# Query-key slabs by seven products, gate slabs drained later, and repeated waits of TensorE removed

## The reference

```python
def _mixer(h, ...):
    z = h @ w_in
    dq, dk, dv, cq, ckv, kr, gl = jnp.split(z, IN_SPLIT_IDX, axis=-1)
    ...
    o_a = _diff_attention(dq..., dk..., dv..., pos, rel_table, lam, lam_init, diff_subln_g)
    o_b = _mla(cq, ckv, kr, pos, mla_q_norm_g, w_uq, mla_kv_norm_g, w_ukv)
    g = jax.nn.sigmoid(gl + b_gate)
    g_a, g_b = g[..., :D_MODEL], g[..., D_MODEL:]
    m = g_a * (o_a @ w_branch_diff) + g_b * (o_b @ w_branch_mla)
    return m @ w_out
```

## Time and profile before

| | us |
|---|---|
| median of 3 runs | 2605.68 (2603.1 to 2606.06) |
| the profiled execution | 2605.08 |
| its span, first to last instruction | 2603.1 |
| TensorE busy | 2518.7 |
| VectorE busy | 1002.7 |
| ScalarE busy | 365.6 |
| GpSimd busy | 130.6 |
| mixer of layer 0, about | 900 to 1185 |
| mixer of layer 1, about | 1421 to 1710 |

### The profile page before, as it was taken

One profiled execution on the slowest core, in us unless ns is written; L12 is line 12 of the kernel. 1 busy time (PEld: TensorE's weight loads), 2 busy tenths in 40 slices (PEclk: granted clock), 3 DMA queues, 4 the chain that ended last, 5 costly groups with the idle time before them and its releaser, 6 DMA issues.

```text
span 2603.1 us, 74060 instructions
## 1 busy us (share of the span) xinstructions
PE 2518.7 (97%) x33806; PEld 2146.4 (82%) x33806; DVE 1002.7 (39%) x1856; ACT 365.6 (14%) x842; POOL 130.6 (5%) x114
## 2 busy tenths in 40 slices
PE   8999999999999999999999999999999999999998
PEld 8966778887698577876994778769999998999997
DVE  5663464633477734444666235440000001000002
ACT  1001241210100023401000234120000001000000
POOL 0000000000100001400000014010000000000000
PEclk9999999999999999999999999999999999999999
DMA  6445242013444542345435323579999999999996
GB/s 260 148 144 196 105 146 110 4 59 130 146 170 150 194 166 82 130 166 209 164 114 197 140 104 129 232 259 368 426 427 426 426 426 401 426 427 426 426 425 256
DMA packets 58054, 607.72 MB, mean 233 GB/s; under 512 B 7365, under 2 KB 7493, under 8 KB 12353
## 3 DMA queue, kind: packets, MB, share of 16 engines
q1 hardware_dynamic: 52272, 587.74, 56.7%
q0 software_dynamic: 5648, 18.04, 2.1%
HBM read 599.66 MB, written 6.09 MB: 233 GB/s over the span
## 4 chain that ended last, share of the span: by engine, by line
PE 90%; DVE 4%; DMA 3%; ACT 2%; issue 1%; SPq 0%; DVEq 0%; ACTq 0%
PE bank L2804 19%; PE bank L314 16%; PE bank L470 16%; PE bank L2817 10%; PE bank L497 7%; PE bank L324 5%; PE bank L1676 3%; PE bank L1798 3%; DMA slot<-in_experts 3%; PE bank L1244 2%; PE bank L1662 1%; DVE arena L2517 1%; PE bank L972 1%; PE bank L2736 1%; PE bank L1267 1%
## 5 line engine op out<-in xcount | busy, mean ns | idle before, releaser
L2804 PE MATMUL bank<-arena,slot 128*64 128x84 f32 x14336 | 540.9, 236 | 12.9 <-issue 7.3
L2804 PEld LDWEIGHTS bank<-arena,slot 128*64 128x64 f32 x14336 | 527.4, 137 | 19.2 <-issue 17.2
L314 PE MATMUL bank<-h_cm,slot 128*128 128x256 f32 x1472 | 324.1, 381 | 0.4 <-ACT h_cm L361 0.2
L314 PEld LDWEIGHTS bank<-h_cm,slot 128*128 128x128 f32 x1472 | 280.1, 191 | 44.4 <-issue 6.5
L3003 DVE TENSOR_TENSOR ff<-ff,bank 128x168 f32<-128x168 f32 x112 | 36.9, 330 | 638.8 <-PE bank L2804 634.6
L2817 PE MATMUL bank<-ff,arena 128*64 128x84 f32 x5376 | 212.8, 238 | 7.6 <-issue 7.2
L2817 PEld LDWEIGHTS bank<-ff,arena 128*64 128x64 f32 x5376 | 202.0, 138 | 13.4 <-issue 13.4
L470 PE MATMUL bank<-arena 128*128 128x128 f32 x1584 | 187.8, 275 | 1.1 <-DVE arena L560 1.1
L470 PEld LDWEIGHTS bank<-arena 128*128 128x128 f32 x1584 | 182.2, 192 | 1.3 <-DVE arena L560 1.3
L314 PE MATMUL bank<-arena,slot 128*128 128x256 f32 x608 | 133.3, 380 | 2.3 <-DVE arena L2520 2.3
L470 PEld LDWEIGHTS bank<-h_cm,slot 128*128 128x128 f32 x1056 | 123.1, 195 | 10.2 <-issue 10.2
(11 more groups left out here) (474 smaller groups left out, 2899.6 us busy)
## 6 DMA issues: line engine op xcount, KB each, us to landing
slot<-in_experts SPq DMA_DIRECT2D x112, 2048.0 KB, 16.1
arena<-in_experts SPq DMA_DIRECT2D x84, 1024.0 KB, 11.8
slot<-in_ffn SPq DMA_DIRECT2D x22, 2048.0 KB, 8.3
x_tm<-in_experts SPq DMA_DIRECT2D x28, 1024.0 KB, 11.6
slot<-in_ffn SPq DMA_DIRECT2D x22, 1024.0 KB, 4.9
slot<-in_dense SPq DMA_DIRECT2D x11, 2048.0 KB, 7.8
slot<-in_dqk SPq DMA_DIRECT2D x8, 2048.0 KB, 7.7
slot<-in_g SPq DMA_DIRECT2D x8, 2048.0 KB, 7.7
```

The source lines that it names most:

```text
L314: ins = pe.matmul(ps[0:m, j * S:(j + 1) * S], w[:, k * width + c0:k * width + c0 + m], rhs[:, k, :], start=k == 0, stop=k == ks - 1)
L2804: ins = pe.matmul(bank[64 * c:64 * c + 64, m * PLACES:(m + 1) * PLACES], weights[:, c0:c0 + 64], CURRENT[:, k, :], start=k == 0, stop=k == ...
```

## The change

- Slabs `dqk(1)` to `dqk(3)` are computed by seven products too, by the functions of the gate slabs, which get a name as argument. Each has a sum slab in `stream` behind it, filled by GpSimd, so that the ring turns three loads further in a layer. TensorE fills four banks for such a slab instead of two, VectorE adds them up and writes q and k, and ScalarE's copies go. `dqk(0)` stays.
- On ScalarE the sigmoids of each gate slab stand later: of slab 0 behind the square of `OA`, of slab 1 behind the exponentials of the second MLA group, of slab 2 behind the square root.
- On VectorE only bank 0 of gate slabs 1 and 2 is drained ahead of the MLA weights, not banks 0 and 1; gate slab 3 is drained as a whole behind the scaling of `OA`, where before its banks 0 and 1 were drained ahead of the reciprocal.
- Waits of TensorE that only repeat an earlier one are gone (`diff_out` of the odd pairs, `mla_scores(1)`, `mla_out(1)`).

```diff
@@ stream @@
+        SEVEN_SLABS = [("dqk_", 1), ("dqk_", 2), ("dqk_", 3)] + [("g2_", n) for n in range(4)]
...
-                if name == "g2_":
-                    stream.append(((f"g2sum_{l}", n), None, 0))
+                if (name, n) in SEVEN_SLABS:
+                    stream.append(((f"sum_{name}{l}", n), None, 0))
@@ pool_slab_sums @@
-            for n in range(4):
-                weights = first_load[f"g2_{l}", n]
-                load, w = gate_sums(l, n)
+            for name, n in SEVEN_SLABS:
+                weights = first_load[f"{name}{l}", n]
+                load, w = slab_sums(l, name, n)
@@ dve_slab_seven @@
+        def slab_tiles(name, n):
+
+            if name == "g2_":
+                return gates2[:, 4 * n:4 * n + 4, :].rearrange("p (g m) s -> p g m s", g=2)
+            return arena[:, 0:4096].rearrange("p (g k s) -> p g k s", g=2, s=S)[:, :, 2 * n:2 * n + 2, :]
@@ pe_mixer2 @@
             def dqk(a):
+                if a:
+                    pe_slab_seven(pe, l, "dqk_", a, SEVEN)
+                    return
...
             def diff_scores(a):
-                for m in range(2):
-                    drained(pe, ("dqk", l, a, m))
+                for key in [("dqk_", l, a, b) for b in (2, 3)] if a else [("dqk", l, 0, m) for m in range(2)]:
+                    drained(pe, key)
...
             def diff_out(a):
...
-                for t in range(T):
-                    drained(pe, ("dv", l, a // 2, t))
+                if a % 2 == 0:
+                    for t in range(T):
+                        drained(pe, ("dv", l, a // 2, t))
@@ act_mixer2 @@
-            dqk(1)
             diff_out(0)
...
-            dqk(2)
             diff_out(1)
...
-            dqk(3)
             diff_out(2)
...
-            g2(0)
             diff_out(3)
             act_softmax(act, l, "mla", 0, 12 * l + 8)
             for a in range(4):
                 drained(act, ("do", l, a))
             act.activation(QD, OA, ACT.Square).then_inc(named("oa_stages"), 1)
-            g2(1)
+            g2(0)
             mla_out(0)
             act_softmax(act, l, "mla", 1, 12 * l + 10)
-            g2(2)
+            g2(1)
             mla_out(1)
             act.wait_ge(named("oa_stages"), 4 * l + 2)
             act.activation(QD, QD, ACT.Sqrt).then_inc(named("oa_stages"), 1)
+            g2(2)
             g2(3)
@@ dve_mixer2 @@
             diff_weights(0)
             latent_norm()
+            dqk(1)
             diff_turned(0)
             diff_weights(1)
+            dqk(2)
             diff_turned(1)
             diff_weights(2)
             rotate()
+            dqk(3)
             diff_turned(2)
...
-            mla_weights(0, lambda: gate(1, 0, 1))
-            gate(1, 2, 3)
+            mla_weights(0, lambda: gate(1, 0))
+            gate(1, 1, 2, 3)
             mla_turned(0)
-            mla_weights(1, lambda: gate(2, 0, 1))
-            gate(2, 2, 3)
+            mla_weights(1, lambda: gate(2, 0))
+            gate(2, 1, 2, 3)
...
             mla_turned(1)
-            gate(3, 0, 1)
             dve.wait_ge(named("oa_stages"), 4 * l + 3)
             ch.step(v.reciprocal(QD, QD))
...
-            gate(3, 2, 3)
+            gate(3, 0, 1, 2, 3)
```

More of the change, by code:

```diff
@@ L1738, in two_blocks, with slab_sums, pool_slab_sums @@
         G_PART = ff[:, 2:4, :].rearrange("p n (u g s) -> p (n u) g s", u=2, g=2)
-        def gate_sums(l, n):
-            load = first_load[f"g2sum_{l}", n]
+        def slab_sums(l, name, n):
+            load = first_load[f"sum_{name}{l}", n]
             return load, [slot[load % SLOTS][:, 1024 * i:1024 * (i + 1)].rearrange("p (k g c) -> p k g c", k=4, g=2)
                           for i in range(4)]
-        def pool_gate_sums(pool, l):
+        def pool_slab_sums(pool, l):
             add, sums = pool.tensor_tensor, named("x_quarters")
@@ L1772, in pool_gate_sums, with slab_product, pe_slab_seven @@
                 add(w[2], quarter_w(s, 0, 0), quarter_w(s, 1, 0), ALU.subtract).then_inc(done, 4)
-        def gate_product(q):
+        def slab_product(q):
             r = SEVEN.index(q)
             return r // 2, slice((r % 2) * S, (r % 2 + 1) * S)
-        def pe_gate_seven(pe, l, n, products):
-            weights = first_load[f"g2_{l}", n]
-            load, w = gate_sums(l, n)
+        def pe_slab_seven(pe, l, name, n, products):
+            weights = first_load[f"{name}{l}", n]
+            load, w = slab_sums(l, name, n)
             s = weights % SLOTS
@@ L1787, in pe_gate_seven @@
             for q in products:
-                b, c = gate_product(q)
-                key = ("g2", l, n, b)
+                b, c = slab_product(q)
+                key = (name, l, n, b)
                 ps = fill(pe, key, next_bank()) if c.start == 0 else PS[job[key][0]]
-                if n == 0 and q == 6:
+                if (name, n) == SEVEN_SLABS[0] and q == 6:
                     pe.wait_ge(named("x_quarters"), 4 * l + 4)
@@ L1801, in pe_gate_seven, with dve_slab_seven @@
             if products[-1] == 3:
[L1802 to L1805 removed]
+                released((f"{name}{l}", n), (name, l, n, 3))
+                released((f"sum_{name}{l}", n), (name, l, n, 3))
+        def slab_tiles(name, n):
+            if name == "g2_":
+                return gates2[:, 4 * n:4 * n + 4, :].rearrange("p (g m) s -> p g m s", g=2)
+            return arena[:, 0:4096].rearrange("p (g k s) -> p g k s", g=2, s=S)[:, :, 2 * n:2 * n + 2, :]
+        def dve_slab_seven(dve, ch, l, name, n, b):
             v = nc.vector
[L1808 removed]
+            ps, tiles = full(dve, (name, l, n, b)), slab_tiles(name, n)
             def product(q):
[L1811 removed]
+                return ps[:, slab_product(q)[1]].rearrange("p (g s) -> p g s", g=2)
             def out(m, j):
[L1814 removed]
+                return tiles[:, :, m, j * P:(j + 1) * P]
             if b == 0:
@@ L1822, in dve_gate_seven @@
             elif b == 2:
-                drained(dve, ("g2", l, n, 1))
+                drained(dve, (name, l, n, 1))
                 v.tensor_tensor(out(1, 0), G_PART[:, 1], product(4), ALU.subtract)
@@ L1827, in dve_gate_seven @@
             else:
-                drained(dve, ("g2", l, n, 2))
+                drained(dve, (name, l, n, 2))
                 ins = v.tensor_tensor(out(0, 1), G_PART[:, 2], product(3), ALU.add)
-            free(ins, ("g2", l, n, b))
+            free(ins, (name, l, n, b))
         P2 = arena[:, 18432:19968].rearrange("p (h s) -> p h s", s=KEYS)
@@ L2166, in mla_scores @@
             def mla_scores(g):
-                pe.wait_ge(named("mla_qk"), 4 * (l + 1))
-                drained(pe, ("krf", l))
-                for b in range(2):
-                    drained(pe, ("uk", l, b))
+                if g == 0:
+                    pe.wait_ge(named("mla_qk"), 4 * (l + 1))
+                    drained(pe, ("krf", l))
+                    for b in range(2):
+                        drained(pe, ("uk", l, b))
                 for t in range(T):
@@ L2193, in mla_out @@
                     drained(pe, ("mt", l, g, b))
-                for t in range(T):
-                    drained(pe, ("uv", l, t))
+                if g == 0:
+                    for t in range(T):
+                        drained(pe, ("uv", l, t))
                 ps = fill(pe, ("mo", l, g), next_bank())
@@ L2312, in g2 @@
                 for b in range(4):
-                    drained(act, ("g2", l, s, b))
+                    drained(act, ("g2_", l, s, b))
                 for tile in range(4 * s, 4 * s + 4):
@@ L2485, in mla_turned, with dqk @@
                 free(v.tensor_copy(PT2.rearrange("p h b s -> p (h b s)")[:, 512:1024], ps[:, :]), ("mt", l, g, 1))
+            def dqk(n):
+                for b in range(4):
+                    dve_slab_seven(dve, ch, l, "dqk_", n, b)
             diff_weights(0)
             latent_norm()
+            dqk(1)
             diff_turned(0)
             diff_weights(1)
+            dqk(2)
             diff_turned(1)
@@ L3264, in _ @@
             for l in range(DEPTH_2):
-                pool_gate_sums(pool, l)
+                pool_slab_sums(pool, l)
                 pool_layernorm(pool, 2 * l)
```

14 lines of the change are left out of this document (4 added, 10 removed).

## The result

The changed kernel takes 2627.6 us (median; 2622.7 to 2628.8), the kernel before 2604.9 beside it. The ratio is 1.0086, 95% interval 1.0074 to 1.0098: 22.6 us slower, where 2601.7 was predicted. The profiled execution took 2626.3 us, its span is 2624.3.

The account below looks back on a forecast made before the run. TensorE, busy for 97% of the span, was taken as the bound: its work, waits and clock. Terms -7.8 -1.0 -7.0 -0.7 +8.5 +4.0 gave -4.0 us: 2601.1 profiled, 2601.7 as median, range 2593 to 2609.

Parts of the forecast that it names:

- The step that failed: Experts, the last third: TensorE and DMA both full, loads started by TensorE's progress, so no gain or loss there.
- Slabs: Three dqk slabs by seven products: 12.51 us each instead of 13.81, saving 7.8 us in two layers.
- scores: Scores after a slab's turning start after 0.73 us instead of 0.89, in six places: 1.0 us gained.
- Sigmoids and weights: Mixers: TensorE's waits at diff output, MLA output and MLA weight turning go, 7.0 us gained in all.
- The stop at `bm` 6: TensorE waits 5.6 us per layer for a bank VectorE drains late; net 4.3 per layer, 8.5 us lost in two.
- The clock: TensorE's clock falls after the `bm` 6 stop: 2.0 us lost per layer, 4.0 in all, ends 3.4 and 5.4.
- Rivals 1 and 2: 1: no stop at `bm` 6, 2589, chance 0.06. 2: stop there but clock stays at 2.4 GHz, 2597.7, chance 0.14.
- The dense start: Dense feed-forward, layer 0 only: TensorE's 0.73 us wait for banks 0 to 3 goes, 0.7 us gained.
- Rival 3: Mixers, weights of heads 6 and 7: GpSimd's sums hold VectorE back, so TensorE waits; slower, 2611.7, chance 0.10.
- Rival 4: Main case with small new waits of 1 to 4 us at a slab's last sum or load: 2602 to 2606, chance 0.10.

Follow-up runs that it names:

- place -57: Changed kernel with TensorE's repeated, already met waits ahead of the experts left out (117 instructions fewer): 2602.9 us, ratio 0.9992.
- the run without them: Changed kernel without TensorE's repeated waits, and with VectorE's first two steps of gate slab 3 ahead of the reciprocal again: 2589.3 us, ratio 0.9949.
- the run where the inner loop is cut too: Kernel before with TensorE's repeated, already met waits left out, 127 instructions fewer: 2865.1 us, ratio 1.0996.
- N = 28: Kernel before with 28 further TensorE instructions (56 waits already met) put in at the very start: 2626.2 us, ratio 1.0078.

## Why the prediction was wrong

- **The step that failed** is the one on the experts: "this stage moves as a whole and neither adds to a gain nor takes from it". It looked at the stage's data and not at its code. What the runs showed in its place: 572 more instructions ahead of the pair loop moved it from 7 pieces over to 8, and its code was fetched anew at three branches back. That was worth 25.3 us in the trace, and 24.6 by the run at place -57; 28 instructions ahead of the kernel before cost 21. No rival held it.
- The costing of the slabs left out a cost of the same kind. It set 56 matmuls of 128 columns against 32 of 256 by their time alone; that these are 96 more instructions in each slab, and that instructions take room, was counted nowhere.
- **Slabs** (-7.8), scores (-1.0): 1.31 us a slab in the trace, and 0.75 us to the scores where 0.73 was taken. By medians the two are 6.3 of 8.8, inside the interval; by the distances in the trace 8.7.
- **Sigmoids and weights** (-7.0): 7.3 by a run of their own, and no wait is left of the three.
- **The stop at `bm` 6** (+8.5): 5.41 us twice against 5.6, so 4.2 net a layer against 4.3.
- **The clock** (+4.0): 2.4 us in layer 0; in layer 1 the same 144 records took 33.9, from 1638.64 to 1672.52, so 2.7. So 5.1, near the upper of the two ends given (5.4). Rivals 1 and 2, no stop and no fall of the clock, are out. Stop and clock together 13.5, and the run without them is 13.6 us faster.
- **The dense start** (-0.7): as forecast, its first record follows the 32 of 13.90 us without a wait. The prediction took the 0.73 for a wait for banks, where the earlier trace rows have "issue"; the wait is gone in every run with the seven-product slabs and there in every other, which fits banks but doesn't show them.

```profile
1201.66 13.90 PE L325 MATMUL bank<-slot,h_cm 128*128 128x512 f32 x32
1215.40 3.73 PE L471 MATMUL bank<-h_cm,slot 128*128 128x128 f32 x32
```

- **Rival 3**, GpSimd in VectorE's way: it came nearer than the waits show. GpSimd is busy for 189.0 us and not 130.6, and the weights of heads 6 and 7 in layer 0 now take, before and then after:

```profile
1036.96 1.01 DVE L2447 TENSOR_SCALAR arena<-arena,ff 128x128 f32<-128x128 f32 x4
```

```profile
1034.66 5.20 DVE L2457 TENSOR_SCALAR arena<-arena,ff 128x128 f32<-128x128 f32 x4
1039.89 5.59 DVE L2462 SCALAR_TENSOR_TENSOR arena<-arena,ff 128x128 f32<-128x128 f32 x4
```

Beside GpSimd's sums these eight operations take 10.8 us, where they took 4.5 before (1.01 and the 3.50 of the earlier trace rows). They end at 1045.48, and the turning stands at 1046.95: 1.5 of the 9.3 us to spare were left. In layer 1 they take 10.8 in place of 2.4, and 1.4 us are left. TensorE waited for none of it, so the term was rightly 0. The 2.1 us that the prediction had for one such meeting were too low a guide, and it hadn't reckoned with the first four operations.

- **Rival 4**, small waits at the slabs: TensorE's list has none on L1799. Out.

The sum was -4.0 at the start of the experts, and it is -4.1 there. The terms as measured add up to -3.2, so that the agreement within 0.1 us is partly luck. The time was wrong all the same, since it ended at the edge of the code that I had read.

Could it have been seen? The place of the loop against the pieces, no: before any run one doesn't know where a piece begins. That the danger was there, yes. In the profile of before the instruction queue brings 36 packets in 900 to 1740 us, then 6 in 1745 to 1800 us and none for the 780 us behind, and a loop of 1681 instructions comes to 6.6 pieces. It lies over 7 of them from 112 places, and a shift by 572, two pieces and 60, leaves these from 60 of the 112: about one chance in two. That is a rival that I left out; its price, 25 us, no row of before gives, but its sign and its chance could have been named.

## What to carry to other kernels

An edit that changes how many instructions stand ahead of a large loop moves that loop against the pieces in which code arrives. Count them (a matmul in fp32 is four here, a transpose two), look at the instruction queue's packets inside the loop, before and after, and when a stage that wasn't touched gets slower with waits for "issue", move the code by some dozens of instructions before you judge the edit. By theory A a loop of at most 6 pieces, 1536 instructions, lies over no more than 7 wherever it begins, so that its place wouldn't matter; that is an estimate, and no run here has such a loop.

## What the runs showed of the hardware

- TensorE's loops run without any fetch at 1681 and 1605 instructions if they lie well: no packet from 1800 to 2580 us in the kernel before. If they don't, a branch back of the pair loop that fetches costs 8.5 to 8.8 us of standing, and in the run where the inner loop is cut too, 15 fetches cost 260 us in all. Not every branch back fetches: two of three with N = 28. The second branch of after stands only 2.31 us: its packets start at 2169.8, while the late gate's matmuls, 14 us of them, still run until 2180.
- A stop for code costs clock as any other does: 1.2 GHz was granted for most of 1957 to 1962 us, behind the stop of 8.80:

```profile
1957.00:1962.00 5.00, 3.75 (x49) 3.65 (x50) 0.00 (x0) 0.00 (x0) 0.00 (x0) 0.54 1.01 423
```

- Two waits that have long been met, in one instruction on TensorE, took 0.11 us: 64, 84 and 128 such instructions put the first matmul at 13.11, 15.31 and 20.22 us, 28 of them at 9.50, where without any it starts at 9.28.
- VectorE operations that read SBUF alone can stand for a whole GpSimd sum. Of the eight at 1034.66 us in after, four take about 0.3 to 0.5 us and every second one 2.4 to 2.6, and those four end 0.1 to 0.3 us behind the ends of GpSimd's four sums (2.35 to 2.5 us each).
